# Two transformer blocks on one core: fewer divided matmuls, and rows of products for the layouts with meta columns

## The reference, cut to what matters

```python
hn = rms_norm_2(h, norm_mix_g)                     # h: 16 meta tokens + 256 tokens
proj = hn @ w_in                                   # 2048 x 12288
u, gb_in, gc_in, v_in, ga_lin, gbr_lin = jnp.split(proj, splits, axis=-1)
pooled = causal_multiscale_pool(u)                 # means over the last 2, 4, 8, 16 tokens
y_a = jnp.einsum("blgc,gcd->blgd", pooled, pool_w).reshape(b, -1, POOL_WIDTH) * pool_scale
y_b = (gb_in * causal_depthwise_conv(gc_in * v_in, conv_w)) @ conv_out_w
h = h + (g_a * y_a + g_b * y_b) @ w_o
h = h + (jax.nn.silu(gate) * up) @ w_down          # the second SwiGLU, f2 below
```

## Time and profile before

| | us |
|---|---|
| median of 3 runs | 2645.22 (2645.04 to 2645.64) |
| the profiled execution | 2644.93 |
| its span, first to last instruction | 2643.1 |
| TensorE matmul busy in the span | 2630.4 |
| VectorE busy | 1571.9 |
| ScalarE busy | 1172.6 |
| mean granted TensorE clock, share of full | 0.999 |

### The profile page before, as it was taken

How to read it: one execution, slowest core, us unless ns; L and a number is a source line. 1 busy time by engine, 2 the same in 40 slices (tenths; PEclk the granted TensorE clock), 3 DMA queues, 4 the chain that set the end, 5 groups by cost and what they waited for, 6 DMA issues and landing times.

```text
span 2643.1 us, 50947 instructions
## 1 busy us (share of the span) xinstructions
PE 2630.4 (100%) x21427; PEld 2568.2 (97%) x21427; DVE 1571.9 (59%) x1557; ACT 1172.6 (44%) x1259; POOL 0.8 (0%) x7
## 2 busy tenths in 40 slices
PE   9999999999999999999999999999999999999998
PEld 7989999999999999999999999999999989998997
DVE  6567765555555556795666666556755555554555
ACT  5446544434443444454433333444554434443444
POOL 0000000000000000000000000000000000000000
PEclk9999999999999999999999999999999999999999
DMA  8644655555655565555555555655555555555553
GB/s 295 197 162 148 204 192 191 191 192 190 194 188 199 189 199 192 177 203 194 176 176 190 179 189 178 201 189 198 191 194 195 199 192 191 190 191 191 190 191 128
DMA packets 254275, 503.33 MB, mean 190 GB/s; under 512 B 8130, under 2 KB 11652, under 8 KB 253988
## 3 DMA queue, kind: packets, MB, share of 16 engines
q1 hardware_dynamic: 252180, 497.61, 56.8%
q10 hardware_dynamic: 1952, 3.68, 0.4%
HBM read 498.37 MB, written 2.88 MB: 190 GB/s over the span
## 4 chain that ended last, share of the span: by engine, by line
PE 99%; DMA 0%; DVE 0%; ACT 0%; SPq 0%; issue 0%; DVEq 0%; ACTq 0%
PE ps L1362 49%; PE ps L1373 24%; PE ps L1391 4%; PE ps L1393 4%; PE ps L1392 4%; PE ps L1409 4%; PE ps L1410 4%; PE ps L1411 4%; PE ps L1401 0%; PE ps L1402 0%; PE ps L1403 0%; DMA xtok<-in_x_dram 0%; PE ps L1360 0%; PE ps L1546 0%; PE ps L1545 0%; PE ps L1544 0%
## 5 line engine op out<-in xcount | busy, mean ns | idle before, releaser
L814 DVE TENSOR_TENSOR lo<-raw,hi 128x1024 fp32r<-128x1024 f32 x940 | 1144.2, 1224 | 931.3 <-ACT hi L487 916.8
L487 ACT ACTIVATE hi<-raw 128x1024 fp32r<-128x1024 f32 x940 | 991.3, 1060 | 1255.8 <-PE ps L1373 945.9
L1362 PE MATMUL ps<-A,hi 128*128 128x256 f32 x7256 | 909.1, 277 | 0.0
L1362 PEld LDWEIGHTS ps<-A,hi 128*128 128x128 f32 x7256 | 863.3, 188 | 0.3
L1362 PE MATMUL ps<-B,hi 128*128 128x256 f32 x3956 | 491.6, 276 | 0.0
L1373 PE MATMUL ps<-A,lo 128*128 128x256 f32 x3648 | 489.3, 277 | 0.0
L1362 PEld LDWEIGHTS ps<-B,hi 128*128 128x128 f32 x3956 | 468.0, 188 | 0.1
L1373 PEld LDWEIGHTS ps<-A,lo 128*128 128x128 f32 x3648 | 448.8, 188 | 0.0
L1373 PE MATMUL ps<-B,lo 128*128 128x256 f32 x1984 | 265.2, 276 | 0.0
L1373 PEld LDWEIGHTS ps<-B,lo 128*128 128x128 f32 x1984 | 243.3, 188 | 0.0
L1410 PE MATMUL ps<-B,hi 128*128 128x258 f32 (+1 forms) x768 | 219.7, 286 | 0.0
(11 more groups left out here) (247 smaller groups left out, 1226.7 us busy)
## 6 DMA issues: line engine op xcount, KB each, us to landing
raw<-in_w_in_dram SPq DMA_DIRECT2D x136, 1024.0 KB, 5.1
raw<-in_ffn_w_dram SPq DMA_DIRECT2D x132, 1024.0 KB, 5.1
raw<-in_w_gate_up_dram SPq DMA_DIRECT2D x88, 1024.0 KB, 5.0
raw<-in_w_down_dram SPq DMA_DIRECT2D x44, 1024.0 KB, 5.0
raw<-in_w_out_dram SPq DMA_DIRECT2D x16, 1024.0 KB, 4.9
raw<-in_pl_w_gate_dram SPq DMA_DIRECT2D x16, 1024.0 KB, 5.0
raw<-in_conv_out_w_dram SPq DMA_DIRECT2D x16, 1024.0 KB, 5.0
raw<-in_w_o_dram SPq DMA_DIRECT2D x16, 1024.0 KB, 5.0
```

The source lines that it names most:

```text
L487: act.activation(hi[:, slot % RING], raw[:, raw_slot, 2 * (slot % 2):2 * (slot % 2) + 2, :], ACT.Copy).then_inc(hi_ready, 1)
L814: dve.tensor_tensor(lo[:, slot % RING], raw[:, slot // 2 % RAWS, 2 * (slot % 2):2 * (slot % 2) + 2, :], hi[:, slot % RING], ALU.subtract). ...
L1362: pe.matmul(ps[:, b0 + m, 0:T], high(slot, kk, m), x, start=j == 0 and kk == 0 and part == 0, stop=False)
```

## The change

TWO_STEPS is gone. Instead a fixed division into columns 0 to 248 and 248 to 256 is made in the fifth matmul of a piece, where a set names the segment and the piece: IN_STEPS_EVER for all turns (`f2_up1` and `f2_up2`, first piece of a turn) and IN_STEPS for a turn whose number `t` is 0 (`f1_up0` piece 8, the first of the second group; the first piece of `plup`, `plgate` and `pool`; `f2_up0` pieces 8 and 12). PT moves by 32 elements in its overlay. The layouts "wide" and "conv" have a function of their own, `with_meta`: it waits for the high weights alone, issues Wh Xh for all eight tiles, then Wh Xl for all eight, waits for the low weights and issues Wl Xh for all eight.

```diff
-TWO_STEPS = {"f1_up0": 128, "f1_down0": 240, "f1_up1": 224, "f1_down1": 192, "f1_up2": 64, "f1_down2": 16, "plgate": 252,
-             "f2_up1": 248, "f2_up2": 8}
+STEP = 248
+IN_STEPS_EVER = {("f2_up1", 0), ("f2_up2", 0)}
+IN_STEPS = IN_STEPS_EVER | {("f1_up0", 8), ("plup", 0), ("plgate", 0), ("pool", 0), ("f2_up0", 8), ("f2_up0", 12)}
...
-        silu_s, UP, PT = overlay(silu_s=[P, MT, T], UP=[P, KT, T], PT=([P, 2, 2 * T], F32R))
+        silu_s, UP, _, PT = overlay(silu_s=[P, MT, T], UP=[P, KT, T], pad_pt=[P, 32], PT=([P, 2, 2 * T], F32R))
...
                         for m in range(MT):
-                            at_col = TWO_STEPS.get(seg.name, 0) if j == 0 and kk == 0 and part == 1 and m == 0 else 0
-                            if at_col:
-                                pe.matmul(ps[:, b0 + m, 0:at_col], high(slot, kk, m), x[:, 0:at_col], start=False, stop=False)
-                                pe.matmul(ps[:, b0 + m, at_col:T], high(slot, kk, m), x[:, at_col:T], start=False, stop=False)
+                            if in_steps and kk == 0 and part == 1 and m == 0:
+                                for a, b in ((0, STEP), (STEP, T)):
+                                    pe.matmul(ps[:, b0 + m, a:b], high(slot, kk, m), x[:, a:b], start=False, stop=False)
...
-                            pe.matmul(to, Wh, Xh, start=first, stop=False, skip_group_check=True)
-                            pe.matmul(to_low, Wh, Xl, start=False, stop=False, skip_group_check=True)
-                            last = pe.matmul(to, Wl, Xh, start=False, stop=final, skip_group_check=True)
...
+            def with_meta(seg, g, j, slot, b0, n):
+
+                ahead = META if seg.reads[1] == "wide" else META - VT0
+                first, final = j == 0, j == seg.pieces - 1
+                pe.wait_ge(hi_ready, n + 1)
+                for kk in range(2):
+                    for m in range(MT):
+                        pe.matmul(ps[:, b0 + m, 0:ahead + T], high(slot, kk, m), B[:, 2 * j + kk, META - ahead:TM],
+                                  start=first and kk == 0, stop=False, skip_group_check=True)
+                for kk in range(2):
+                    for m in range(MT):
+                        pe.matmul(ps[:, b0 + m, ahead:ahead + T + ahead], high(slot, kk, m), B[:, 2 * j + kk, TM:TM + T + ahead],
+                                  start=False, stop=False, skip_group_check=True)
+                pe.wait_ge(lo_ready, n + 1)
+                for kk in range(2):
+                    for m in range(MT):
+                        last = pe.matmul(ps[:, b0 + m, 0:ahead + T], low(slot, kk, m), B[:, 2 * j + kk, META - ahead:TM],
+                                         start=False, stop=final and kk == 1, skip_group_check=True)
                 last.then_inc(pieces_used, 1)
...
-                            if not two_passes(seg, g):
+                            if seg.reads[1] == "wide" or seg.reads[1] == "conv" and not two_passes(seg, g):
+                                with_meta(seg, g, j, slot, b0, n)
+                            elif not two_passes(seg, g):
                                 piece(seg, g, j, slot, b0, n)
                             else:
-                                highs(seg, g, j, slot, b0, n)
+                                highs(seg, g, j, slot, b0, n, (seg.name, g * seg.pieces + j) in (IN_STEPS if t == 0 else IN_STEPS_EVER))
                                 lows(seg, g, j, slot, b0, n)
```

More of the change, by code:

```diff
@@ L1344, in two_passes, with highs @@
                 return layout in ("halves", "wide_halves") or (layout == "conv" and seg.kinds[g] == "cb")
-            def highs(seg, g, j, slot, b0, n):
+            def highs(seg, g, j, slot, b0, n, in_steps):
                 buf, layout, _ = seg.reads
@@ new lines, in piece @@
+                        Xh, Xl = X[:, k, 0:T], X[:, k, T:2 * T]
+                        to = ps[:, b0 + m // 2, (m % 2) * T:(m % 2 + 1) * T]
+                        pe.matmul(to, Wh, Xh, start=first and m % 2 == 0, stop=False, skip_group_check=True)
+                        pe.matmul(to, Wh, Xl, start=False, stop=False, skip_group_check=True)
+                        last = pe.matmul(to, Wl, Xh, start=False, stop=final, skip_group_check=True)
+                last.then_inc(pieces_used, 1)
+            def with_meta(seg, g, j, slot, b0, n):
[15 more added lines that the diff above has]
+                                         start=False, stop=final and kk == 1, skip_group_check=True)
```

## The result

| | before | after |
|---|---|---|
| median, us | 2645.22 (2645.04 to 2645.64) | 2679.09 (2678.88 to 2679.49) |
| profiled execution, us | 2644.93 | 2678.88 |
| its span, us | 2643.1 | 2677.1 |
| matmuls in the trace | 21427 | 21387 |

A forecast was written before the change was run, and what follows sets the result against it. TensorE's distance between matmul starts was taken as the bound. Divisions (9.8 us) plus rows of products (5.1) gave 14.9 us off, so 2630.3 us from the median of 2645.22; range 2619.5 to 2640.

The forecast's parts named there:

- What bounds the kernel, and the two rates: TensorE alone bounds; one matmul shape runs fast or slow at one clock, 2.720 or 2.827 us a piece, 0.107 apart.
- Entered slow, 248 and 8 columns lead to fast: A division at column 248 turns a slow stretch fast, costing 0.15 us; in f1_up0 a gain of 0.87 us was forecast.
- All of these groups are entered fast, so nothing is lost by not dividing: f1_down0 to f1_down2, 200 pieces: dropping all divisions gains 3.11 us.
- The padding of PT: Moving PT by 128 bytes makes plup fast: gain 0.31 us, or a loss of 0.11 if place does not matter.
- `plgate` without a division: The division named for plgate never runs, as the segment has no peeled turn: 12 divisions, gain 0.46 us.
- `pool`: One division, entered slow, costs 0.15 us and makes the segment fast: gain 0.70 us.
- `f2_up1` and `f2_up2`: Divisions on the first group of each turn leave these segments fast: gains of 0.46 and 3.73 us.
- `f2_up0`: Two divisions, 0.15 and 0.11 us, replace four slow pieces costing 0.43: gain 0.17 us.
- The rows of products: u2, cv and cg: eight tiles on one operand instead of hi, hi, lo per tile gain 5.1 us, a third of 15.4.
- The upper bound of 15.4: u2, cv and cg at the fast rate in proportion to width; as a rival 2620.0 us, chance 0.21.
- a side remark of a rival: Rows of cg leave cb slow, and 104 pieces up to f2_up0: 14 us; chance within 0.10 shared with slower rows.
- The slower rival: f1_up0 stays slow behind the side product, 255 pieces to the end of f1_down2: 27 us, 2657.5 us, chance 0.07.

The follow-up runs named there:

- e1: The changed kernel with one division, in the first piece of f1_up0's second group, set back from column 248 to 128: 2647.08 us, ratio to before 1.0007.
- b1: The changed kernel with column 128 in f1_up0 piece 8, f2_up0 piece 8 and the cb groups, no divisions in plup, pool, f2_up0 piece 12: 2632.99 us.
- n1: b1 without the seven divisions in f2_up1 and f2_up2 and with PT where it was before: 2644.58 us.
- w1: b1 with start column and width varied in the rows of u2, cv and cg, output not the reference's; distances between starts were read, no total time given.
- e2: The kernel before with only the rows of products (with_meta) added: 2655.89 us, ratio 1.004.

## Why the prediction was wrong

**What bounds the kernel, and the two rates**: right. All that moved was the distance between matmuls, at one clock and with no new wait, and 0.107 us a piece carried the whole loss: 0.1067 x 200 is 21.3, and `f1_down0` to `f1_down2` grew by 18.2 plus the 3.1 us of divisions that they no longer had.

**"Entered slow, 248 and 8 columns lead to fast"**: this is the step that failed. It rested on one slow entry, behind a token segment. In the kernel after, 248 mended the two entries behind token segments, and met three others, in `f1_up0`, `plup` and `f2_up0` piece 8, where it failed each time. The row beside it warned of it: 8 and 248 columns failed twice and mended twice. A column that acts both ways on what looks the same says that something is not seen. I took it as a mark of that column only. What the runs show in its place: whether a division mends depends on its column and on where in the three matmuls of the slow stretch it falls, and 248 fails in one place of the three. It was to be had from the trace of before: where 8 mended in `f2_up2` (2458.20 and 2525.53 us) the long distance was the last, where it failed at 2502.81 the last but one, and in `f1_up0` at 366.59 it was the last, the place where 248 then failed. The gain of 0.87 in `f1_up0` became a loss of 5.1, and the whole stretch lost 27.1.

**"All of these groups are entered fast, so nothing is lost by not dividing" (3.11)**: true of the kernel before, and no longer true once `f1_up0` stayed slow. It was a gain on a condition, entered in the sum as a sure one, with `plgate` (0.46) and `plup` (0.31) behind the same condition. In e1 and b1, where the condition holds, all three come out as worked out: 544.00, 87.04, 10.88 and one division.

**The padding of PT**: right, shown by n1. **`plgate` without a division**: right; only 12 of the 13 run. **`pool`**: 0.74 gained for the 0.70 forecast, by another way; the rows of `u2` leave TensorE fast, and the division entered there costs 0.11 and mends nothing. **`f2_up1` and `f2_up2`**: right, 0.45 and 3.73 for 0.46 and 3.73. **`f2_up0`**: it lost 0.6 for a gain of 0.17, since the stretch ahead of it came in slow and 248 failed behind its side product.

**The rows of products (a third of 15.4, 5.1 us)**: they gave 0.84 in `u2` and 1.68 in `cv` and `cg`, 2.5. The reason given was half right: in `u2` the low operand's row runs at 123.7 ns, those of the high operand still at 126.3 and 126.7. In `cv` and `cg` the three are alike, 119.6 to 120.5. The upper bound of 15.4 was never to be had, because width is not paid in proportion: 272 columns take 123.3 ns from the better of two starts, and 258 take 120.8 from the same start (w1) and 120.0 from column 14 (the kernel after). And it had a consequence that I put into a side remark of a rival: their end leaves `cb` slow and all up to `f2_up0` with it: 3.3, 10.2 and 0.4, 14.0 us in e2. The three weights of the interleaved order had left it fast.

**The slower rival** named both mechanisms and both places, at 2657.5 and some 14 us, which stack to 2672. The measured 2679 is higher since the first stretch runs on to the side product of `ga`, not to the end of `f1_down2` (4.6 us), and since the rows gave 2.6 less than forecast. I gave 0.07 to the long stretch and a part of 0.10 to the short one. The argument against, one mended entry, deserved much less: a stretch of 255 pieces without a second chance, 300 as it came, hung on it.

**What stays open**: what a slow stretch is inside TensorE. The runs show that it goes round in threes, at which places a division ends it, and that starts in memory matter; not by which part. Why a plain float32 product begins a slow stretch in `f1_up0` and ends one in `ga`, and why the rows of `cg` begin one, is not shown. The Trainium skill, "TensorE: Matmul & The Clock Gate", section "Part 2: What happens when you issue a matmul", gives the moving operand and the weights independent read ports; the 6.7 ns that a start column costs show that the place of the moving operand is not free beside a weight load, but not that the weight load is the reason. No run tried that apart.

## What to carry to other kernels

Where TensorE is the bound, take the time of a repeated unit from the trace, stretch by stretch, before anything else: two rates for one shape at one clock mean a state that can be entered and left, and here it is worth 4%. A repair that acts on such a state is tested at each place where it is to stand, for slow stretches that look alike in their rate answer differently; and a cheap repair that is repeated (0.11 us a group) insures against a stretch of hundreds of units, so take the repetitions out only after each single one has been seen to hold. Changing the order of matmuls in one segment can be paid for in the next four.

## What the hardware showed that was not expected

- A slow stretch of 256-column float32r matmuls (117.8 ns instead of 113.3) goes on through 300 pieces, segment changes and loops, with no side step in it and two divisions that failed (`f1_up0`, `plup`), and is the same in every kernel here that had one: 2.827 us a piece.
- A slow stretch has a period of three matmuls: distances of 117.50, 117.50 and 118.33 ns. In 264 divisions entered slow, no pair of column and place in the three has two outcomes; 248 fails where the long distance is the last ahead of it (11 of 11), 128 in none of the three (50 of 50 mended).
- 256 columns of B from column 16 take 113.3 ns, from column 0 or 14 take 120.0; PT moved by 128 bytes changes `plup` from 117.8 to 113.3.
- 240 columns take 112.0 ns against 113.3 for 256: below 256 columns hardly anything is saved, and above them 258 cost 120.8.
